# Attention of a two-layer encoder step: the four narrow query tiles of a head transposed and multiplied as one run

## The reference

```python
sc = (jnp.einsum('bqhd,bshd->bhqs', qn, k_nope)
      + jnp.einsum('bqhe,bse->bhqs', qr, kr)).astype(jnp.float32) * MLA_SCALE
sc = jnp.where(kchunk[None, :] <= qchunk[:, None], sc, NEG)
pr = jax.nn.softmax(sc, axis=-1).astype(v.dtype)
return jnp.einsum('bhqs,bshd->bqhd', pr, v)
```

## Time and profile before

| | |
|---|---|
| median of three runs | 3078.17 us |
| the profiled execution's own time | 3077.48 us |
| its span on the core | 3075.7 us |
| busy in the span: PE, PEld | 95%, 91% |
| busy in the span: VectorE, GpSimd, ScalarE | 66%, 53%, 41% |
| mean granted clock of PE | 0.971 of full speed |

### The profile page before, as it was taken

One profiled execution on the slowest core, in us unless ns is written; L12 is line 12 of the kernel. 1 busy time (PEld: TensorE's weight loads), 2 busy tenths in 40 slices (PEclk: granted clock), 3 DMA queues, 4 the chain that ended last, 5 costly groups with the idle time before them and its releaser, 6 DMA issues.

```text
span 3075.7 us, 55101 instructions
## 1 busy us (share of the span) xinstructions
PE 2912.2 (95%) x18226; PEld 2799.1 (91%) x18226; DVE 2020.0 (66%) x3893; ACT 1247.8 (41%) x2651; POOL 1620.5 (53%) x1239
## 2 busy tenths in 40 slices
PE   7899999989999999998989899999899999999987
PEld 7888888988999999998878888889899999999887
DVE  4646998366666666667575489964766666666775
ACT  4225777244322322225352177753522232232452
POOL 4223555566545545546454455554754554554663
PEclk9999999999999999998999999999899999999999
DMA  3496554320111111112103566532211111111301
GB/s 117 154 321 208 126 126 93 118 84 35 44 59 41 45 57 41 49 65 102 49 15 140 171 155 152 134 82 71 82 43 60 42 44 58 41 48 55 129 32 57
DMA packets 174144, 272.58 MB, mean 89 GB/s; under 512 B 96128, under 2 KB 122256, under 8 KB 173520
## 3 DMA queue, kind: packets, MB, share of 16 engines
q1 hardware_dynamic: 174032, 271.11, 29.0%
HBM read 201.32 MB, written 69.87 MB: 88 GB/s over the span
## 4 chain that ended last, share of the span: by engine, by line
PE 62%; issue 14%; POOL 12%; DVE 7%; ACT 2%; DMA 2%; SPq 1%; POOLq 0%; DVEq 0%; ACTq 0%
PE ps L1558 27%; PE ps L1209 10%; PE ps L1211 10%; PE ps L1210 10%; POOL probs L1034 8%; PE ps L1498 2%; DVE sublayer_out L2408 1%; DVE act_lo L2423 1%; PE ps L1230 1%; POOL pre_sums L991 1%; PE ps L1244 1%; DVE pre_sums L2384 1%; DVE post_sums L2384 1%; DMA kA_lo<-stage_lo 1%; DVE stage_lo L2507 1%
## 5 line engine op out<-in xcount | busy, mean ns | idle before, releaser
L2661 DVE TENSOR_TENSOR sublayer_out<-ps,sublayer_out 128x352 f32<-128x352 f32 x1008 | 527.2, 524 | 477.6 <-PE ps L1211 474.5
L1209 PE MATMUL ps<-act_hi,weight_hi 128*128 128x352 f32 (+2 forms) x1344 | 457.9, 341 | 31.2 <-DVE weight_lo L2452 11.5
L1034 POOL TENSOR_TENSOR probs<-probs,row_inv 128x1024 f32<-128x1024 f32 (+8 forms) x288 | 312.2, 1094 | 287.3 <-DVE row_inv L2593 287.0
L1210 PE MATMUL ps<-act_lo,weight_hi 128*128 128x352 f32 (+2 forms) x1344 | 444.0, 330 | 0.0
L1211 PE MATMUL ps<-act_hi,weight_lo 128*128 128x352 f32 (+2 forms) x1344 | 443.9, 330 | 0.0
L1558 PE MATMUL ps<-act_hi,weight_lo 128*128 128x352 f32 x1280 | 413.8, 323 | 0.0
L1558 PE MATMUL ps<-act_hi,weight_hi 128*128 128x352 f32 x1280 | 413.3, 323 | 0.0
L1558 PE MATMUL ps<-act_lo,weight_hi 128*128 128x352 f32 x1280 | 412.9, 323 | 0.0
L969 POOL TENSOR_TENSOR weight_lo<-weight_raw,weight_hi 128x1024 fp32r<-128x1024 f32 x111 | 274.1, 2469 | 220.4 <-ACT weight_hi L1983 203.3
L1112 POOL TENSOR_TENSOR weight_lo<-weight_raw,weight_hi 128x512 fp32r<-128x512 f32 x160 | 205.1, 1292 | 248.3 <-ACT weight_hi L2066 248.3
L1209 PEld LDWEIGHTS ps<-act_hi,weight_hi 128*128 128x128 f32 (+2 forms) x1344 | 259.5, 193 | 40.2 <-issue 24.3
(11 more groups left out here) (223 smaller groups left out, 7533.3 us busy)
## 6 DMA issues: line engine op xcount, KB each, us to landing
weight_raw<-units SPq DMA_DIRECT2D x199, 512.0 KB, 3.7
k_hi<-kB_hi SPq DMA_DIRECT2D x32, 328.0 KB
residual_kept<-residual SPq DMA_DIRECT2D x6, 1408.0 KB, 7.1
residual<-residual_kept SPq DMA_DIRECT2D x6, 1408.0 KB, 10.5
kA_hi<-stage_hi SPq DMA_DIRECT2D x8, 656.0 KB, 3.0
kA_lo<-stage_lo SPq DMA_DIRECT2D x8, 656.0 KB, 4.7
k_hi<-kA_hi SPq DMA_DIRECT2D x16, 328.0 KB
k_lo<-kA_lo SPq DMA_DIRECT2D x16, 328.0 KB
```

The lines of the kernel that those rows point to most:

```text
L1034: pool.tensor_tensor(p, p, rinv[0:M, k:k + 1].to_broadcast((M, KEYS[tile])), ALU.mult).then_inc(at_p, 1)
L1209: nc.tensor.matmul(out, ah, bh, start=first, stop=False)
L1210: nc.tensor.matmul(out, ah, bl, start=False, stop=False)
L2661: V.tensor_tensor(y[:, m, c], src, y[:, m, c], ALU.add).then_inc(f_acc, 1)
```

## The change

Tiles 0 to 3 become one run, `(0, 1, 2, 3)`, in place of `(0, 1)` and `(2, 3)`. Its chunks go by key blocks: chunk 8 is key block 0 for the four tiles, chunk 9 key block 1 for tiles 1 to 3, chunk 10 key block 2 for tiles 2 and 3 and key block 3 for tile 3. There are as many chunks as before, at the same steps, and the same ten blocks to transpose; chunk 8 has four in place of three, chunk 9 three in place of four. A value product goes over all blocks of one key block in its chunk: 512 columns in chunk 8, 384 in chunk 9, 256 and 128 in chunk 10.

```diff
-RUNS = [(6, 7), (8,), (4, 5), (0, 1), (2, 3)]
+RUNS = [(6, 7), (8,), (4, 5), (0, 1, 2, 3)]
...
-def blocks_of(run):
+def chunks_of(run):
 
     if run == (8,):
-        return [(k, 8) for k in range(3)]
-    a, b = run
-    return [(k, t) for k in range(b) for t in (a, b)] + [(b, b)]
-
-
-CHUNKS = []
-for _run in RUNS:
-    _all = blocks_of(_run)
-    CHUNKS += [(_run, _all[_k:_k + 4], _k == 0, _k + 4 >= len(_all)) for _k in range(0, len(_all), 4)]
+        return [[(k, 8) for k in range(3)]]
+    rows = [[(k, t) for t in run if t >= k] for k in range(run[-1] + 1)]
+    if len(run) == 2:
+        every = sum(rows, [])
+        return [every[k:k + 4] for k in range(0, len(every), 4)]
+    return rows[:-2] + [rows[-2] + rows[-1]]
+
+
+def flagged(run):
+
+    every = chunks_of(run)
+    return [(run, x, k == 0, k == len(every) - 1) for k, x in enumerate(every)]
+
+
+CHUNKS = sum([flagged(_run) for _run in RUNS], [])
...
-    if run == (0, 1):
+    if run == (0, 1, 2, 3):
         return 3 * hp + PART_OF[8] + 1
...
-                        for j in range(0, len(of), 2):
-                            kt, tile = of[j]
-                            mm = products(kt, j, min(2, len(of) - j), tile, P, P)
+                        for kt, row in itertools.groupby(enumerate(of), lambda x: x[1][0]):
+                            row = list(row)
+                            mm = products(kt, row[0][0], len(row), row[0][1][1], P, P)
```

More of the change, by code:

```diff
@@ L11 @@
+import itertools
 from contextlib import ExitStack
```

## The result

The changed kernel takes 3141.09 us, the median of four runs (3138.51 to 3145.32), against 3078.0 us; the ratio is 1.0209, 95% interval [1.0195, 1.0222]. The prediction was 3150 us, with 3118 to 3176 as its range. The profiled execution took 3145.32 us.

A forecast was written before the change was run, and what follows sets the result against it. PE's queue paced layer 0, PE and VectorE layer 1, with the chain maximum, exponential, scores tight. Profiled 3077.48 us plus 48.3 (late exponential) plus 24 (clock) made 3149.8; with 0.7 for the median, 3150 us, range 3118 to 3176.

The forecast's parts named there:

- What bounds the kernel: In the attentions, PE paces layer 0, PE and VectorE layer 1; PE has no slack for a later maximum of tile 5.
- Part one, the merged products: Value products of chunks 8 and 9: four matmuls fewer a head save 0.09 us, counted as nothing before PE's wait.
- The starts: Start-to-start times of PE's matmuls: 0.23 us for 512 columns, 0.12 for 256, used to size the merging.
- Part two, the later start: At handovers, tile 0's exponential waits for chunk 10's turn, delaying tile 5's maximum and tile 1's scores: 48.3 us in all.
- Part three, the earlier wait for tile 3: Chunk 8 now waits for GpSimd's product on tile 3, with some 2.2 us to spare: priced at nothing.
- Part four, the clock: PE idles some 1.8 us before tile 1's scores; its clock falls in 16 of 30 gaps, 1.5 us each: 24 us.
- the prediction's two rows: Trace rows on PE's clock: it held after 1.34 us idle, was at the lower level after 1.65 us.

The follow-up runs named there:

- run 1: The changed kernel, but last_turn goes by a chunk's blocks, so tile 0's exponential waits for chunk 8 again: 3070.19 us, ratio 0.998 to the kernel before.
- Run 5: run 1 with chunk 9 turned at step 13 instead of 12, putting tile 5's maximum ahead of chunk 9's low part on VectorE: 3071.43 us, ratio 0.9977.
- run 3: run 1 with the value products of chunks 8 and 9 cut into pieces of at most two blocks: 3070.73 us, ratio 0.9983.
- run 4: The changed kernel plus ten matmuls of 384 columns adding zeros, on PE behind chunk 9's value product: 3124.88 us, ratio 1.0163.
- run 2: The kernel before, with only tile 0's exponential made to wait for the turn of chunk 10: 3146.76 us, ratio 1.0232.

## Why the prediction was right, and where a size was off

- *What bounds the kernel.* Right: the chain maximum of tile 5, exponential, scores of tile 1 has no slack for something later. In layer 0, from the first head of a pair to the second, a lateness forecast at 1.97 us made the head 1.90 us longer (17.44 to 19.34 us), and the 0.24 us that run 1 won made it 0.22 us shorter. In layer 1 the 0.32 and 0.28 us that run 1 won brought 0.28 and 0.16. Run 5 adds how far this reaches: it brings the exponential of tile 5 forward by 0.97 us, but by an order that puts low parts behind the maximum of tile 5, and these then hold PE up by as much.
- *Part one, the merged products.* The starts were right as such: the product of chunk 8 in run 1 goes from 394.00 to 394.55 (rows below), 0.55 us, where 0.54 was worked out. The prediction counted none of the 0.09 us a head, for the wait behind it; run 3 shows that this holds even without the late wait, in the 0.08 us by which PE's wait there is shorter.

PE in run 1, the merged product of chunk 8 and the scores behind it:

```profile
394.00 0.48 PE L1413 MATMUL ps<-probs_t_hi,v_both 128*128 128x512 f32 x1
394.31 0.40 PE L1413 MATMUL ps<-probs_t_lo,v_both 128*128 128x512 f32 x1
394.55 0.40 PE L1216 MATMUL ps<-k_hi,q_hi 104*128 104x512 f32 x1
```

- *Part two, the later start.* Right in its steps, with one of them too long. The exponential of tile 0 starts 0.53 us after the turn of chunk 10 (407.91 to 408.44), as forecast; the high part of chunk 9 follows 0.36 us later instead of 0.51, the low part 0.51 after that, where 0.50 was forecast. The sum over the 30 handovers was 48.3 us. By the heads whose clock held, the four kinds of handover cost 1.90, 1.49, 1.63 and 1.26 us (forecast 1.97, 1.49, 1.70 and 1.21), 47.5 us in all; run 4 leaves 48.5.
- *Part three, the earlier wait for tile 3.* Right: no turn of the changed kernel waits for GpSimd in either window.
- *Part four, the clock.* The mechanism and the size of the gap were right: forecast 1.8 us, measured 1.65 and 1.79 in layer 0, 1.73 and 1.87 in layer 1. The number of falls, 18 for 16, came out close by luck: 16 was a choice between bounds of 0 and 30 from two rows, and run 2 has 12 of 30 in gaps that are little shorter. The term that was mis-sized is the price of one: forecast 1.7 and 1.3 us, 1.5 on average; measured on the length of the heads 1.45 and 1.08 in layer 0 (by the kind of handover), 1.10 and 0.44 in layer 1, and in run 2 nearly the same, 1.44 and 1.08, 1.07 and 0.46. The 16 falls that have another handover behind them made the heads of the changed kernel 15.4 us longer in all. So the term is 14 to 16 us where 24 stood, and that is nearly all of the 9 us by which the forecast lies too high.

A fall does last as long as the one it was read from (0.51 over 3.40 us; the earlier trace rows). What failed is the step from there to half of 3.4 us. PE in the changed kernel behind two gaps of one kind, first that of 412.66 above, where the clock held, then one where it fell, each down to the next scores of 384 columns:

```profile
412.88 0.28 PE L1217 MATMUL ps<-k_lo,q_hi 104*128 104x256 f32 x1
413.00 0.28 PE L1218 MATMUL ps<-k_hi,q_lo 104*128 104x256 f32 x1
...
415.04 0.34 PE L1216 MATMUL ps<-k_hi,q_hi 104*128 104x384 f32 x1
```

```profile
452.81 0.55 PE L1216 MATMUL ps<-k_hi,q_hi 104*128 104x256 f32 x1 [1.65 <-ACT probs L1943]
453.16 0.42 PE L1217 MATMUL ps<-k_lo,q_hi 104*128 104x256 f32 x1
453.38 0.41 PE L1218 MATMUL ps<-k_hi,q_lo 104*128 104x256 f32 x1
...
456.65 0.34 PE L1216 MATMUL ps<-k_hi,q_hi 104*128 104x384 f32 x1
```

From the end of the gap it is 2.38 us to these scores where the clock held and 3.84 where it fell: PE is 1.46 us late when the clock is back, not 1.7, and in this kind of handover it stays as late to the end of the head. At the lower level the next start comes 0.22 us after that of a matmul of 256 columns, against 0.12, which is less than twice. In the other kind of layer 0 PE is 1.16 us late when the clock is back, in layer 1 it is 1.40 and 1.11; of these 0.08, 0.30 and 0.67 come back before the next handover. Which of PE's waits give that back was not followed up, and neither was what makes one gap bring a fall and another none.

The Trainium skill (TensorE: Matmul & The Clock Gate, section HAM oscillation — how this bites in real kernels), by which the clock would hold in gaps as short as these, is not borne out here: it fell behind 18 of 30 of them, and run 4, which has none, shows no fall in either of these windows.

## What to carry to other kernels

When items are put into larger groups, look for every wait that is worked out from the group: a wait for the last of the group costs each member that was through earlier. Here a merging worth less than 3 us brought a wait that cost 63 us, and the same merging with the wait by item is 6 to 10 us faster than the kernel before, through a copy that it happened to shorten. And a wait taken off one engine pays only up to the next thing that is late; read that from the queue of the engine that feeds it.

## What the runs showed of the hardware that was not expected

- The same idle time goes either way. Gaps of 1.65 us of the same place in layer 0 were followed by a fall in some heads and by none in others of one execution (412.66 and 452.81 above). The idle of 1.34 us ahead of layer 0's attention, behind which the clock held in the trace of before, is 1.35 us in run 1, and there the clock fell behind it; the row and a window of run 1:

```profile
268.50 0.32 PE L1216 MATMUL ps<-k_hi,q_hi 104*32 104x288 f32 x1 [1.35 <-ACT probs L1943]
```

```profile
270.20:273.60 3.40, 3.40 (x16) 3.04 (x14) 1.77 (x4) 1.32 (x4) 3.03 (x4) 0.51 0.00 0
```

So the prediction's two rows, one held and one fallen, mark no border. Whether one gap brings a fall can't be told from its length: it was 12 of 30 at 1.54 to 1.62 us in run 2, 18 of 30 at 1.65 to 1.87 in the changed kernel.
- More work was faster. Ten matmuls of 384 columns in each gap, 2.00 us of PE's time each time, took 14 to 16 us off the program, and the clock stayed at its upper level.
- Widths scaled as the starts said: one product of 512 columns takes 0.24 us to the next start, two of 256 take 0.24. Wider products from 256 columns on saved PE nothing here.
